# Block-2 key, value and gate-column weights loaded into another buffer than the weight ring

## The chip, the cores and the metric

The kernel runs on one core of a Trainium2 chip. The metric is the device time of one execution in microseconds (us). Weights are read from the chip's memory in single precision; nothing is resident between executions.

## What is computed

Two transformer-like blocks, one after the other, on 256 latent tokens of width 1024 (the first block also carries 256 context tokens). The change lies in the second block, which has two layers, each with weights of its own. Cut to what matters:

```
h = rms_norm_2(x, norm_mix[l]) * (1.0 + sc1) + sh1
proj = h @ w_in[l]                       # 1024 x 7440
dn_qkv, dn_z, dn_a, dn_b, sw_q, sw_k, sw_v, gate_a, gate_b = _split_columns(proj, IN_SIZES)
dn_qkv = silu(causal_dwconv(dn_qkv, dn_conv[l]))      # 3072 columns
g, beta = gates from dn_a, dn_b                       # 8 + 8 columns
o_dn = gated_delta_rule_chunked(dq, dk, dv, g, beta)
sq, sk = partial_rope(rms_norm_2(sw_q ...)), partial_rope(rms_norm_2(sw_k ...))
y_b = swa_sink_attention(sq, sk, sv, swa_sinks[l]) @ w_swa_out[l]    # sw_k, sw_v: 128 + 128 columns
merged = sigmoid(gate_a) * y_a + sigmoid(gate_b) * y_b
x = x + gt1 * (merged @ w_o[l])
x = x + gt2 * ((silu(up_act) * up_lin) @ w_down[l])
```

## The kernel before

The program of every engine is written out by hand, and engines meet only at semaphores. A planner (`make_plan`) walks the stages once and numbers two things: the *jobs* (one PSUM bank filled by TensorE and emptied by ScalarE or VectorE) and the *tiles* of the weight ring.

**The ring.** `ring` has two slots (`RING = 2`) of 2 MB each. A weight tile of a `weights` stage takes a whole slot, whatever its width; a weight tile of the feed-forward part takes half a slot. SyncE (SP) issues all weight loads in program order (`load`, L608 to L619). Before each load it waits until the tile that last filled the slot was used: for whole tiles, until the jobs of that tile are complete (`acc_full`). So the tile after next can be loaded only when the present one is finished. TensorE waits in `weights` (L708) until its slot has landed.

**The order in the second block.** Each layer begins with `norm`, and then, in this order: two query tiles of 512 columns (`swa_q`), the key tile of 128 columns (`swa_k`), the value tile of 128 columns (`swa_v`), six tiles of 512 columns for the delta rule (`dn_in`), and one tile of 16 columns (`dn_ab`). Queries, keys, values and the 16 columns go through `by_token` (TensorE line L763); the six tiles go through `by_feature` (L775), four blocks of 256 tokens each per tile, and VectorE convolves each block as it comes (L2710 to L2714). After that come the transposes (L1324), the attention with `dn_z` products filled in between (L789), and the rest of the layer. The layer ends with the feed-forward part (`seven_products`, TensorE line L724), which makes sums of the weights on VectorE (L2453 to L2456) and reads 22 up pairs and then 12 down chunks from half slots.

**Around the feed-forward part on SP.** After the loads of the 22 up pairs (`up_pairs`) SP issues eleven small loads of per-layer vectors (`layer_rows`) and then the down chunks (`down_chunks`), each of which waits for a half slot. For the first block's second feed-forward part these are the vectors of layer 0, for layer 0's they are those of layer 1.

**The slab buffer.** `mod_w`, 128 partitions of 2 x 2048 numbers, takes the slabs of the modulation matrices (SP line L598) while the first block runs; VectorE multiplies them (L2106) and counts them in `mod_used`. The last of the 88 slabs loaded there is used in the first block, before its second feed-forward part. Nothing in the second block touches `mod_w`.

Of the kernel before, what the change touches and what calls it, by code (L numbers as in the profile page):

```python
# [14 lines left out]
P = 128  # L15
D = 1024
KD = D // P
# [229 lines left out]
def make_plan():  # L247
    a = Plan()
    a.slab_tiles("modA", 2)
    a.free_jobs("xT", KD)  # L250
    a.slab_tiles("modA2", 2)
    a.free_jobs("norm0", 1)

    def tiles(where, stages, engine="A"):
        job = 0
        for name, jobs in stages:
            a.start(name)
            for n in jobs:
                for left in range(n, 0, -1):
                    a.add(name, engine[(n - left) % len(engine)])  # L260
                    if left == 1:
                        a.tile_used()
                    job += 1

    tiles("even", (("even_q", [4]), ("even_k", [4]), ("even_v", [4]), ("even_bi", [4]), ("even_bg", [4])))
    a.free_jobs("even_qkT", 2 * NT)
    a.use_banks(0, 1)
    for slot in range(SLOTS):
        for h, t in heads_at(slot):
            if t == 15:  # L270
                a.free_jobs(f"hg_o{h}", 1)
        for j, k in fill_at(slot):
            if (j, k) == (0, 0):
                a.start(f"head{slot // PER_ROUND}")
            if k == 0:
                a.add(f"head{slot // PER_ROUND}", "A")
            if (j, k) == (2, KD - 1):
                a.tile_used()
        if slot == CAT_SLOT:
            a.free_jobs("att_catT", KD // 2)  # L280
            a.start("even_out_a")
        if PART_SLOT <= slot < PART_SLOT + KD:
            a.add("even_out_a", "V")
            if slot == PART_SLOT + KD - 1:
                a.tile_used()
    a.use_banks(2, 3, 0, 1)
    a.free_jobs("hg_catT", KD // 2)
    a.weights("even_out", [KD], "V")
    first = a.tile["even_q"]
    a.slab_tile = [first + 2 * (3 * i // 2 // 4) for i in range(MOD_EARLY)] + [first + 2 * ((13 + i // 2) // 4) for i in range(KD)]  # L290
    a.free_jobs("norm1", 1)
    a.sevens("ffn0", "down0")
    a.slab_tile += [a.tile["ffn0"] + q - 1 for q in range(KF) for _ in range(up_slabs(q))]
    a.slab_tile += [a.tile["down0"] + n for n in range(4 * len(CHUNKS)) for _ in range(DOWN_SLABS[n])]
    a.free_jobs("norm2", 1)
    tiles("odd", (("ret_q", [4, 4]), ("ret_k", [4, 4]), ("ret_v", [4] * 4), ("ret_g", [2] * 4)))
    a.slab_tile += [a.tile["ret_q"] + n for n in (2, 2, 2, 2, 4, 4, 4, 4, 4, 6, 6, 6, 6, 6, 6, 8, 8, 8, 10, 10, 10, 12, 12, 12,
                                                  14, 14, 14, 16)]
    a.free_jobs("ret_oT", KD)
    a.pairs("ret_out", 1)  # L300
    a.free_jobs("norm3", 1)
    a.sevens("ffn1", "down1")
    assert len(a.slab_tile) == KD * (len(MOD_GROUPS) - 1)

    for l in range(2):
        a.free_jobs(f"norm@{l}", 1)
        a.weights(f"swa_q@{l}", [2, 2])
        a.weights(f"swa_k@{l}", [2])
        a.weights(f"swa_v@{l}", [2])
        a.weights(f"dn_in@{l}", [4] * 6, "V")  # L310
        a.weights(f"dn_ab@{l}", [2])
        a.free_jobs(f"swa_qkT@{l}", 6)
        a.weights(f"dn_z@{l}", [2, 2])
        a.free_jobs(f"swa_oT@{l}", KD)
        a.weights(f"swa_out@{l}", [2, 2])
        a.weights(f"gate_b@{l}", [2, 2])
        a.weights(f"gate_a@{l}", [2, 2])
        a.free_jobs(f"dn_oT@{l}", KD)
        a.weights(f"dn_out@{l}", [2, 2], "V")
        a.free_jobs(f"mergeT@{l}", KD)  # L320
        a.weights(f"w_o@{l}", [4, 4], "V")
        a.free_jobs(f"norm_ffn@{l}", 1)
        a.sevens(f"up@{l}", f"down@{l}")
    return a
# [39 lines left out]
def first_then_second_block(nc, a, out):  # L364
    pl = make_plan()
    DEPTH2 = a["w_in_2"].shape[0]

    with ExitStack() as ctx:
# [122 lines left out]
        def half_tile(n, k):  # L491

            return ring[:, n // 2 % RING, 2048 * (n % 2):2048 * (n % 2) + 256 * k].rearrange(
                "p (k e n) -> p k e n", e=2, n=256)

        rv, rg, rk, rq = view(0, 4, 2048), view(8192, 2, 2048), view(12288, 8, 512), view(16384, 8, 256)
        r_t = view(18432, 2, 2, 256)
        r_P, r_D, r_junk = view(19456, 2, 4, 256), view(21504, 2, 4, 256), gate[:, 0, 0:512]
# [30 lines left out]
        w_in = [sem(f"weights{s}_in") for s in range(RING)]  # L529
        h_in = [sem(f"half_weights{s}_in") for s in range(2 * RING)]  # L530
        w_part = sem("weights_partly_used")
        st_ws, st_ts = sem("st_weight_sums"), sem("st_input_sums")
        st_p1, st_p6, st_p7, st_p2, st_x, st_z = (sem(f"st_{n}") for n in (
            "product1", "product6", "product7", "product2", "x_full", "z_full"))
# [44 lines left out]
        def _(sp):  # L579
# [83 lines left out]
            for c in range(12):  # L663
                load(wcols(a["odd_w_in"][0], 512 * c, 512 * c + 512))
            down(a["odd_w_out"][0], (16,))
            up_pairs(a["ffn_w_in"][1])
            layer_rows(0)
            down_chunks(a["ffn_w_out"][1])
            for l in range(DEPTH2):
                w = a["w_in_2"][l]  # L670
                for lo, n in ((4112, 512), (4624, 512), (5136, 128), (5264, 128), (0, 512), (512, 512), (1024, 512),
                              (1536, 512), (2048, 512), (2560, 512), (4096, 16), (3072, 512), (3584, 512)):
                    load(wcols(w, lo, lo + n))
                for h in range(2):
                    load(wcols(a["w_swa_out_2"][l], 512 * h, 512 * h + 512))
                for lo in (6416, 6928, 5392, 5904):
                    load(wcols(w, lo, lo + 512))
                for name in ("w_dn_out_2", "w_o_2"):
                    for h in range(2):
                        load(wcols(a[name][l], 512 * h, 512 * h + 512))  # L680
                up_pairs(a["w_up_2"][l])
                if l + 1 < DEPTH2:
                    layer_rows(l + 1)
                down_chunks(a["w_down_2"][l])
            assert tile.n == pl.tiles and slab.n == len(pl.slab_tile)

# [8 lines left out]
        def _(pe):  # L695
# [57 lines left out]
                    if k == KD - 1:  # L753
                        fresh[0] = None

            def by_token(tiles, width, src=hT, where=None):

                w = weights(width)
                for i in tiles:
                    b = bank()  # L760
                    for k in range(KD):
                        first_use(k)
                        ins = nc.tensor.matmul(b[:, 0:width], src[:, k, P * i:P * (i + 1)], w[:, k, :],  # L763
                                               start=k == 0, stop=k == KD - 1)
                    ins.then_inc(acc_full, 1)
                    mod_after(where)
# [538 lines left out]
            for l in range(DEPTH2):  # L1305
# [2 lines left out]
                norm(4 + 2 * l, 256, "norm")  # L1308
                for _ in range(2):
                    by_token(LAT, 512)  # L1310
                for _ in range(2):
                    by_token(LAT, P)
                for _ in range(6):
                    by_feature(4, 256, 512)
                by_token(LAT, 16)

                stage("swa_qkT")
                for i in range(2):
# [1540 lines left out]
```

## Time and profile before

| what | value |
|---|---|
| median of 3 executions | 2884.79 us (2884.76, 2884.79, 2913.66) |
| profiled execution | 2885.55 us, of which the span is 2883.4 us |
| mean granted TensorE clock in the profiled execution | 0.969 of full speed |
| TensorE busy | 2720.8 us, 94% of the span |
| VectorE busy | 1542.3 us, 53% |
| ScalarE busy | 669.5 us, 23% |
| moved from the chip's memory | 383.96 MB, 134 GB/s over the span |

The span is the time from the first to the last recorded event of one profiled execution. All other times are read in it as us from its start. A busy TensorE isn't TensorE at its peak: in some stretches the clock granted to it is half of the full one, and then the same work keeps it busy for twice as long.

### The profile page before, as it was taken

What the parts mean: (1) busy time and instruction counts of PE and PEld (TensorE: products, weight loads), DVE (VectorE), ACT (ScalarE), POOL (GpSimd) and SP (SyncE); (2) the same over time, 40 slices, a digit from 0 to 9 for tenths busy, and PEclk for the clock granted to TensorE, in tenths of its full rate; (3) what the DMA queues carried; (4) which work ended last, traced back from release to release, by engine and by line L of the source; (5) the groups of instructions that cost most, each with busy time, mean ns of one, the idle gap of its engine ahead of it and who ended that gap; (6) DMA issues with size and microseconds to landing.
All of it is one profiled execution on the core that took longest, in us unless ns stands there. A gap on an engine that the chain in (4) does not pass through costs nothing.

```text
span 2883.4 us, 36232 instructions
## 1 busy us (share of the span) xinstructions
PE 2720.8 (94%) x14426; PEld 2050.3 (71%) x14426; DVE 1542.3 (53%) x3100; ACT 669.5 (23%) x1727; POOL 0.2 (0%) x4
## 2 busy tenths in 40 slices
PE   6899988999999999899999999989998999998999
PEld 2445555888887444589977756668996864775999
DVE  4856555755775521136745554425773654443775
ACT  3134322111102100212111351222311144222330
POOL 0000000000000000000000000000000000000000
PEclk9998889999999999999999999999999999999999
DMA  7530012555475844145634221124553322113554
GB/s 291 200 94 23 34 55 88 175 161 171 174 282 199 304 165 163 59 130 164 181 131 151 97 88 59 59 88 130 164 182 127 134 88 88 59 59 101 154 168 134
DMA packets 336164, 387.36 MB, mean 134 GB/s; under 512 B 10988, under 2 KB 265084, under 8 KB 323452
## 3 DMA queue, kind: packets, MB, share of 16 engines
q1 hardware_dynamic: 333260, 378.15, 39.9%
q10 hardware_dynamic: 2736, 6.89, 0.7%
q8 instruction: 115, 1.88, 0.3%
q14 instruction: 53, 0.43, 0.0%
HBM read 383.96 MB, written 1.05 MB: 134 GB/s over the span
## 4 chain that ended last, share of the span: by engine, by line
PE 86%; DVE 6%; DMA 3%; ACT 3%; issue 2%; ACTq 0%; SPq 0%; DVEq 0%
PE acc L724 24%; PE acc L763 12%; PE acc L775 11%; PE mx L724 10%; PE acc L789 8%; PE acc L1031 2%; PE acc L1016 2%; PE acc L805 2%; PE mx L1409 1%; PE mx L1398 1%; PE mx L1407 1%; DVE arena L2106 1%; PE mx L889 1%; PE mx L1291 1%; PE acc L821 1%
## 5 line engine op out<-in xcount | busy, mean ns | idle before, releaser
L763 PE MATMUL acc<-ring,hT 128*128 128x512 f32 (+2 forms) x1152 | 407.6, 515 | 19.3 <-DMA ring<-in_even_w_in 9.5
L763 PEld LDWEIGHTS acc<-ring,hT 128*128 128x128 f32 x1152 | 197.9, 194 | 226.2 <-issue 207.6
L724 PE MATMUL acc<-arena 128*128 128x128 f32 (+1 forms) x2056 | 322.6, 299 | 2.1 <-ACT gate L1817 0.8
L775 PE MATMUL acc<-hT,ring 128*128 128x256 f32 (+1 forms) x1280 | 311.5, 407 | 12.8 <-DMA ring<-in_w_in 8.1
L775 PEld LDWEIGHTS acc<-hT,ring 128*128 128x128 f32 x1280 | 246.9, 193 | 76.5 <-issue 33.8
L724 PEld LDWEIGHTS acc<-arena 128*128 128x128 f32 x2056 | 282.8, 192 | 16.1 <-ACT gate L1817 1.4
L2106 DVE SCALAR_TENSOR_TENSOR arena<-mod_w,vcols,arena 128x2048 f32<-128x2048 f32 x98 | 228.4, 2348 | 110.4 <-DMA mod_w<-in_w_ada 100.9
L789 PE MATMUL acc<-ring,hT 128*128 128x512 f32 x512 | 258.0, 625 | 1.1 <-ACT hT L1496 1.1
L724 PE MATMUL acc<-hT,ring 128*128 128x128 f32 (+1 forms) x1208 | 194.9, 311 | 12.1 <-ACT hT L1586 12.0
L2453 DVE TENSOR_TENSOR arena<-ring 128x512 f32<-128x512 f32 (+1 forms) x136 | 91.6, 674 | 192.6 <-PE acc L724 184.7
L724 PEld LDWEIGHTS acc<-hT,ring 128*128 128x128 f32 x1208 | 171.6, 197 | 26.5 <-issue 11.8
L724 PE MATMUL acc<-arena,ring 128*128 128x128 f32 (+1 forms) x1160 | 182.4, 300 | 1.9 <-DVE x L2594 1.9
L724 PEld LDWEIGHTS acc<-arena,ring 128*128 128x128 f32 x1160 | 159.7, 192 | 10.4 <-DVE x L2594 2.7
L1496 ACT ACTIVATE arena<-acc 128x512 f32<-128x512 f32 (+2 forms) x136 | 69.8, 527 | 414.2 <-PE acc L763 293.4
L789 PEld LDWEIGHTS acc<-ring,hT 128*128 128x128 f32 x512 | 91.4, 196 | 89.7 <-issue 84.4
L724 PE MATMUL mx<-hT,ring 128*128 128x128 f32 (+1 forms) x928 | 151.0, 307 | 0.0
L724 PE MATMUL mx<-arena,ring 128*128 128x128 f32 (+1 forms) x928 | 148.5, 302 | 0.0
L724 PEld LDWEIGHTS mx<-hT,ring 128*128 128x128 f32 x928 | 132.5, 196 | 6.5
L724 PEld LDWEIGHTS mx<-arena,ring 128*128 128x128 f32 x928 | 128.7, 191 | 9.0 <-issue 3.4
L724 PE MATMUL acc<-hT,arena 128*128 128x128 f32 (+1 forms) x760 | 124.7, 307 | 0.0
L724 PEld LDWEIGHTS acc<-hT,arena 128*128 128x128 f32 x760 | 108.3, 191 | 6.0
L1031 PE MATMUL acc<-hT,ring 128*128 128x512 f32 x192 | 99.7, 659 | 0.0
(355 smaller groups left out, 3441.0 us busy)
## 6 DMA issues: line engine op xcount, KB each, us to landing
ring<-in_w_in SPq DMA_DIRECT2D x28, 2048.0 KB
mod_w<-in_w_ada SPq DMA_DIRECT2D x48, 1024.0 KB, 5.9
ring<-in_ffn_w_in SPq DMA_DIRECT2D x88, 512.0 KB
ring<-in_w_up SPq DMA_DIRECT2D x88, 512.0 KB
mod_w<-in_mod_w SPq DMA_DIRECT2D x40, 1024.0 KB, 5.0
ring<-in_odd_w_in SPq DMA_DIRECT2D x12, 2048.0 KB
ring<-in_ffn_w_out SPq DMA_DIRECT2D x16, 1024.0 KB
ring<-in_w_down SPq DMA_DIRECT2D x16, 1024.0 KB
```

The source lines that it names most:

```text
L724: ins = nc.tensor.matmul(out, w[:, k, :], h[:, k, :], start=start and k == 0, stop=stop and k == n - 1, skip_group_check=more)
L763: ins = nc.tensor.matmul(b[:, 0:width], src[:, k, P * i:P * (i + 1)], w[:, k, :], start=k == 0, stop=k == KD - 1)
L775: ins = nc.tensor.matmul(b[:, 0:hi - lo], w[:, k, P * f:P * (f + 1)], hT[:, k, lo:hi], start=k == 0, stop=k == KD - 1)
L789: ins = nc.tensor.matmul(filling.b, src[:, k, P * i:P * (i + 1)], filling.w[:, k, :], start=k == 0, stop=k == KD - 1)
L805: ins = nc.tensor.matmul(b[:, 0:width], w[:, k, P * f:P * (f + 1)], src[:, at + k, :], start=at + k == 0, stop=at + k == sum(groups) - 1)
L821: ins = nc.tensor.transpose(b[:, at:at + P], src[:, i, P * (k + q):P * (k + q + 1)], ident)
L889: nc.tensor.matmul(mx[:, u % 2, 0:P * blocks], q, k, start=True, stop=True).then_inc(att_s, 1)
L1016: ins = nc.tensor.matmul(b, w[:, k, P * f:P * (f + 1)], hT[:, first + k, :], start=k == 0, stop=k == 3)
L1031: ins = nc.tensor.matmul(hb, hw[:, kk, P * j:P * (j + 1)], hT[:, kk, :], start=kk == 0, stop=kk == KD - 1)
L1496: ins = nc.scalar.activation(dst, src, func, **kw)
L2106: ins = V.scalar_tensor_tensor(acc_, mod_w[:, i % 2, :], vcols[:, at:at + 1], acc_, ALU.mult, ALU.add)
L2453: V.tensor_tensor(s3, a11, a10, ALU.subtract)
```

## The change

The key and value columns of one layer, which are neighbours in `w_in`, are loaded by one transfer of 128 x 8 x 256 numbers (1 MB) into the first half of `mod_w`, and the 16 gate columns by one of 128 x 8 x 16 numbers (64 KB) into its second half. Both are issued by SP at the previous feed-forward part, between its up pairs and its down chunks: for layer 0 ahead of the small vectors, for layer 1 behind them. TensorE waits for a semaphore of their own (`small_in`) once a layer, ahead of the key product. The three ring tiles of each layer are gone; the jobs, the products and the order of TensorE's work stay.

```diff
@@ make_plan
-        a.weights(f"swa_k@{l}", [2])
-        a.weights(f"swa_v@{l}", [2])
+        a.free_jobs(f"swa_k@{l}", 2)
+        a.free_jobs(f"swa_v@{l}", 2)
         a.weights(f"dn_in@{l}", [4] * 6, "V")
-        a.weights(f"dn_ab@{l}", [2])
+        a.free_jobs(f"dn_ab@{l}", 2)
@@ views
+        kv_w = mod_w[:, 0, :].rearrange("p (k n) -> p k n", k=KD)
+        ab_w = mod_w[:, 1, 0:P].rearrange("p (k n) -> p k n", k=KD)
@@ SP
+            def small_weights(l):
+                if l:
+                    sp.wait_ge(acc_full, pl.own[f"dn_ab@{l - 1}"][-1] + 1)
+                else:
+                    sp.wait_ge(mod_used, KD * (len(MOD_GROUPS) - 1))
+                sp.dma_start(kv_w, wcols(a["w_in_2"][l], 5136, 5392)).then_inc(small_in, 16)
+                sp.dma_start(ab_w, wcols(a["w_in_2"][l], 4096, 4112)).then_inc(small_in, 16)
             up_pairs(a["ffn_w_in"][1])
+            small_weights(0)
             layer_rows(0)
             down_chunks(a["ffn_w_out"][1])
...
-                for lo, n in ((4112, 512), (4624, 512), (5136, 128), (5264, 128), (0, 512), (512, 512), (1024, 512),
-                              (1536, 512), (2048, 512), (2560, 512), (4096, 16), (3072, 512), (3584, 512)):
+                for lo, n in ((4112, 512), (4624, 512), (0, 512), (512, 512), (1024, 512),
+                              (1536, 512), (2048, 512), (2560, 512), (3072, 512), (3584, 512)):
                     load(wcols(w, lo, lo + n))
...
                 if l + 1 < DEPTH2:
                     layer_rows(l + 1)
+                    small_weights(l + 1)
@@ TensorE
-                for _ in range(2):
-                    by_token(LAT, P)
+                pe.wait_ge(small_in, 32 * l + 32)
+                for v in range(2):
+                    by_token(LAT, P, w=kv_w[:, :, P * v:P * (v + 1)])
                 for _ in range(6):
                     by_feature(4, 256, 512)
-                by_token(LAT, 16)
+                by_token(LAT, 16, w=ab_w)
```

SP's queue at layer 0, from the last load of a query tile on (`in_w_in_2` is the matrix `w_in` of the second block; 128x8x512 is a 2 MB tile, 128x8x128 the key or value tile, 128x8x16 the gate columns). Before:

```order
L616 DMA ring<-in_w_in_2 128x8x512 [waits st_down_product,weights_partly_used]
L616 DMA ring<-in_w_in_2 128x8x128 [waits acc_full] x2
L616 DMA ring<-in_w_in_2 128x8x512 [waits acc_full] x6
L616 DMA ring<-in_w_in_2 128x8x16 [waits acc_full]
L616 DMA ring<-in_w_in_2 128x8x512 [waits acc_full] x2
L616 DMA ring<-in_w_swa_out_2 128x8x512 [waits acc_full] x2
```

And after the change:

```order
L619 DMA ring<-in_w_in_2 128x8x512 [waits st_down_product,weights_partly_used]
L619 DMA ring<-in_w_in_2 128x8x512 [waits acc_full] x8
L619 DMA ring<-in_w_swa_out_2 128x8x512 [waits acc_full] x2
```

The first `dn_in` tile now stands directly behind the second query tile, so that it waits for the jobs of the first query tile and no longer for those of the key tile.

SP's queue in the first block's second feed-forward part, at the end of the up pairs (`in_ffn_w_in`) and the start of the down chunks (`in_ffn_w_out`), after the change:

```order
L619 DMA ring<-in_ffn_w_in 128x8x128
L674 DMA mod_w<-in_w_in_2 128x8x256 [waits mod_slabs_used]
L675 DMA mod_w<-in_w_in_2 128x8x16
L657 DMA prow<-in_dn_conv_2 96x128
...
L661 DMA brow<-in_dn_norm_2 128x128
L619 DMA ring<-in_ffn_w_out 128x8x256 [waits st_z_full] x2
```

The two rows with `mod_w` are new; before, the row with `prow` followed the up pair directly.

## Rows read from the trace of the kernel before

**Rows 1.** The page: its span, TensorE's busy time, the chain by engine.

```profile
span 2883.4 us, 36232 instructions
PE 2720.8 (94%) x14426; PEld 2050.3 (71%) x14426; DVE 1542.3 (53%) x3100; ACT 669.5 (23%) x1727; POOL 0.2 (0%) x4
PE 86%; DVE 6%; DMA 3%; ACT 3%; issue 2%; ACTq 0%; SPq 0%; DVEq 0%
```

**Rows 2.** Waits of TensorE from 1495 us on: total us, times, longest us.

```profile
PE mx L1367 <- DVE arena L2767: 10.3, 2, 5.1
...
PE acc L775 <- DMA ring<-in_w_in: 8.1, 2, 4.4
...
PE acc L763 <- DMA ring<-in_w_in: 0.9, 2, 0.4
```

**Rows 3.** Timeline of TensorE, start of layer 0: start, us, what, [idle before <-releaser].

```profile
1495.04 33.99 PE L763 MATMUL acc<-ring,hT 128*128 128x512 f32 x96 [2.16 <-ACT hT L1586]
1529.45 3.84 PE L763 MATMUL acc<-ring,hT 128*128 128x128 f32 x32 [0.41 <-DMA ring<-in_w_in]
1536.98 84.83 PE L775 MATMUL acc<-hT,ring 128*128 128x256 f32 x384 [3.69 <-DMA ring<-in_w_in]
1621.65 3.64 PE L763 MATMUL acc<-ring,hT 128*128 128x16 f32 x32
```

**Rows 4.** Timeline of TensorE, start of layer 1.

```profile
2225.49 3.84 PE L763 MATMUL acc<-ring,hT 128*128 128x128 f32 x32 [0.45 <-DMA ring<-in_w_in]
2233.75 84.83 PE L775 MATMUL acc<-hT,ring 128*128 128x256 f32 x384 [4.42 <-DMA ring<-in_w_in]
```

**Rows 5.** Timeline of SP at layer 0, issues without their waits.

```profile
1511.81 0.39 SPq L616 DMA_DIRECT2D ring<-in_w_in  x1
...
1525.54 3.96 SPq L616 DMA_DIRECT2D ring<-in_w_in  x2
```

**Rows 6.** Windows around the two waits: stretch, us, busy by engine, PEclk, DMA share, GB/s.

```profile
1533.30:1537.00 3.70, 0.02 (x1) 0.02 (x1) 0.00 (x0) 3.40 (x5) 0.00 (x0) 1.00 1.06 392
1537.00:1540.00 3.00, 3.00 (x10) 2.45 (x11) 0.00 (x0) 0.00 (x0) 0.00 (x0) 0.68 1.05 390
1540.00:1543.00 3.00, 3.00 (x12) 2.55 (x11) 0.54 (x2) 0.00 (x0) 0.00 (x0) 0.75 0.53 194
...
2233.80:2236.80 3.00, 3.00 (x9) 2.42 (x10) 0.00 (x0) 0.00 (x0) 0.00 (x0) 0.60 1.04 388
2236.80:2239.80 3.00, 3.00 (x13) 2.59 (x12) 0.57 (x2) 0.00 (x0) 0.00 (x0) 0.83 0.29 104
```

**Rows 7.** Windows: a 2 MB tile, the gate columns, first down chunks with the pause ahead.

```profile
1595.20:1601.40 6.20, 6.20 (x31) 5.45 (x30) 3.18 (x8) 0.83 (x2) 0.00 (x0) 1.00 0.96 338
1609.00:1610.00 1.00, 1.00 (x7) 0.87 (x6) 0.93 (x3) 0.00 (x0) 0.00 (x0) 1.00 0.70 66
1405.80:1408.50 2.70, 2.70 (x27) 2.70 (x26) 1.46 (x6) 0.55 (x2) 0.00 (x0) 1.00 0.13 29
1408.50:1413.00 4.50, 4.50 (x42) 4.50 (x42) 3.62 (x6) 0.86 (x4) 0.00 (x0) 1.00 0.73 245
2103.70:2107.70 4.00, 4.00 (x38) 4.00 (x37) 3.17 (x8) 1.44 (x4) 0.00 (x0) 1.00 0.77 261
```

**Rows 8.** Timeline of VectorE: convolution of the first two dn_in blocks, layer 0.

```profile
1542.43 0.48 DVE L2710 TENSOR_SCALAR arena<-acc,pcols 128x256 f32<-128x256 f32 x1 [9.24 <-PE acc L775]
...
1545.88 0.48 DVE L2710 TENSOR_SCALAR arena<-acc,pcols 128x256 f32<-128x256 f32 x1 [1.42 <-PE acc L775]
```

**Rows 9.** Timeline of VectorE: first use of the first down chunk, both feed-forward parts.

```profile
1415.85 0.68 DVE L2453 TENSOR_TENSOR arena<-ring 128x512 f32<-128x512 f32 x1
...
2112.16 0.68 DVE L2453 TENSOR_TENSOR arena<-ring 128x512 f32<-128x512 f32 x1
```

**Rows 10.** Timeline of TensorE: its first product with the first down chunk.

```profile
1418.94 1.06 PE L724 MATMUL mx<-arena,ring 128*128 128x128 f32 x8
```

**Rows 11.** Windows of one place in layer 0 and its counterpart in layer 1.

```profile
1730.00:1742.00 12.00, 9.65 (x20) 4.86 (x20) 3.12 (x14) 1.55 (x7) 0.00 (x0) 0.72 0.01 1
2427.00:2439.00 12.00, 9.65 (x27) 4.58 (x27) 3.90 (x16) 2.14 (x8) 0.00 (x0) 1.00 0.04 3
```

More of the change, by code:

```diff
@@ L531, in first_then_second_block @@
         w_part = sem("weights_partly_used")
+        small_in = sem("small_weights_in")
         st_ws, st_ts = sem("st_weight_sums"), sem("st_input_sums")
@@ L754, in first_use, with by_token @@
                         fresh[0] = None
-            def by_token(tiles, width, src=hT, where=None):
-                w = weights(width)
+            def by_token(tiles, width, src=hT, where=None, w=None):
+                w = weights(width) if w is None else w
                 for i in tiles:
```

## The prediction

> **What bounds the kernel now.** I read the page first. TensorE is busy for 94% of the span and carries 86% of the chain that ended last [rows 1]. So time comes back only where TensorE stands idle or runs at a low clock, and the next view is the list of what it waited for. In the second block, the waits for weights in the ring are 8.1 us ahead of L775, in two pieces, and 0.9 us ahead of L763, in two pieces [rows 2]. The larger entry ahead of them, 10.3 us, is a wait for VectorE in the delta rule; the change doesn't touch it.
>
> Then the timeline says where the pieces are. In layer 0 the query products start at 1495.04. The key product follows them without a pause. The value product, at 1529.45, had to wait 0.41 us for its tile. It ends at 1533.29, and then TensorE stands for 3.69 us until the first `dn_in` tile has landed at 1536.98 [rows 3]. Layer 1 shows the same, with 0.45 and 4.42 us [rows 4]. The product of the 16 gate columns, at 1621.65, had no wait at all [rows 3].
>
> SP's queue says why. At 1511.81, when the first query tile is used up, it issues the key tile. At 1525.54, when the second is used up, it issues the value tile, and the next issue in that row ends at 1525.54 + 3.96 = 1529.50 [rows 5]: this is the first `dn_in` tile, which had to wait until the key jobs were complete. From 1529.5 to 1536.98 are 7.5 us for 2 MB, and the transfer engines run at their full share meanwhile (1.06 at 392 GB/s) [rows 6]. Nothing is slow there. The load starts too late, because a 0.5 MB tile held a 2 MB slot.
>
> **Part 1: the three tiles leave the ring.** The first `dn_in` tile now waits for the first query tile, so it is issued at 1511.8. A 2 MB tile takes 6.2 us of transfer [rows 7]; with the 7.5 us from issue to landing seen above it is there at 1519.3. It is needed when the value product ends, at 1533.3 less 0.4. That leaves some 13 us. The second tile is issued when the second query tile is used up, at 1525.5, and lands at 1533.0, while its turn comes 13.8 us after the first tile's start (four blocks of 3.45 us: VectorE gets the first at 1542.43 and the second at 1545.88 [rows 8]). So it has some 13 us too. From there on each tile has 13.8 us for a load of 7.5. The waits of 3.69 and 0.41 us go whole, and nothing in the ring is late next.
>
> **Part 2: the clock behind the wait.** TensorE's granted clock is 1.00 during the wait of 3.7 us, and then 0.68 and 0.75 in the two stretches of 3 us behind it: part of the time it ran at the lower level (1.2 of 2.4 GHz). What this lost is 3 x 0.32 + 3 x 0.25 = 1.71 us. In layer 1 it is 3 x 0.40 + 3 x 0.17 = 1.71 us [rows 6]. With the wait gone TensorE is busy without a pause from 1495.04 on, and I take it that the clock stays up. VectorE's start fits this: the first block took 1542.43 - 1536.98 = 5.45 us against 3.45 for the next [rows 8], of which the 1.71 is the greater part.
>
> **Part 3: who else must keep up.** VectorE waited 9.24 us ahead of the first block and 1.42 us ahead of the second [rows 8]. It needs 2.0 us of each 3.45, so it follows an earlier TensorE. Every later wait in the layer is one of an engine for another's work that itself begins earlier. They move with TensorE and don't grow. The gate columns cost nothing before and cost nothing after.
>
> **Part 4: the added loads.** In both feed-forward parts SP issues two more transfers, at some 0.39 us each as in [rows 5], 0.8 us in all, and the transfer engines move 1.06 MB more. The nearest row for the 1 MB is the first down chunk, of the same shape and size: at 245 GB/s over 4.5 us (3.3 us of full share) [rows 7]. The gate columns took 0.7 of 1 us at 66 GB/s [rows 7]. Together this is 4.0 us of transfer per layer, queued ahead of the first down chunk, whose issue moves by 0.8 us as well. That chunk landed by 1413.0 and VectorE first read it at 1415.85 [rows 7, 9]; in layer 0's part it landed by 2107.7 and was read at 2112.16 [rows 7, 9]. So it has 2.9 and 4.5 us to spare before anyone starts later. In the first case the transfer engines were nearly idle for 2.7 us before the chunk (share 0.13 [rows 7]), and this absorbs most of the 4.0 us; in both, TensorE's own first use is 3.1 us behind VectorE's (1418.94 [rows 10]). The lower bound of the cost is therefore nothing, and the upper is the whole of what exceeds the spare time with no gap absorbed: 4.8 - 2.9 = 1.9 us once and 0.3 us once, 2.2 us in all. I take nothing, since VectorE's lead over TensorE stands behind the first margin. The new waits on SP (the slabs used, the gate jobs of layer 0 complete) were met long before; nothing is queued behind them that would feel it. TensorE's new wait for `small_in` comes some 120 us after the issue.
>
> On the DMA order, the Trainium skill (DMA: Bandwidth & Descriptors, Queues, rings and completion order) says that each DMA engine takes the descriptors of one ring in their order. By that rule the down chunk must indeed stand behind the whole 1.06 MB, which is how the bound above is drawn; by a rule without order it would be less.
>
> **The sum.** Layer 0: 0.41 + 3.69 + 1.71 = 5.81 us. Layer 1: 0.45 + 4.42 + 1.71 = 6.58 us. Together 12.4 us. The profiled execution took 2885.55 us, 0.8 us above the median of 2884.79. Against its own time the changed kernel would take 2873.2; I give the forecast against the median: 2884.8 - 12.4 = 2872.4 us.
>
> **Rivals.**
> *The clock falls elsewhere.* The loss at low clock is not tied to the program alone. At one place in layer 0 (1730 to 1742) the mean clock is 0.72, at its counterpart in layer 1 (2427 to 2439) it is 1.00, with the same 9.65 us of busy time in the same 12 us [rows 11]. That is 12 x 0.28 = 3.4 us in one and none in the other. If all that follows begins 5 to 12 us earlier, such places can change sides. About ten pauses follow; with one or two changed by 3.4 us or by half of it, the forecast moves by up to 5 us to either side: 2867 to 2878. That all of them go one way and eat half of the gain or more (2878 to 2882), or add as much (2863 to 2867), is possible too. For it speaks the pair of rows; against it, that flips should cancel. The Trainium skill (TensorE: Matmul & The Clock Gate, The HAM clock gate) says that the check of activity runs freely and isn't reset by the kernel; by that rule a shift alone re-deals these losses, and the trace agrees, as far as one pair of places can show.
>
> *The wait moves.* If the first `dn_in` tile were no longer late but something behind it were, for instance VectorE, which also norms and rotates the queries between the blocks, part of the 8.1 us would return. Half of it back gives 2884.8 - 6 = 2879. Against it speaks that TensorE has no wait of size between 1536.98 and 1621.65 (84.83 us in one piece [rows 3]).
>
> *Slower.* The early loads could hold up the down chunks. The point from which this decides: to end above the old time the two chunks must together cost TensorE more than 12.4 us, so each must land some 6 us beyond its spare time, that is 9 to 11 us later than now, for 4.8 us of added queue. It needs transfers of 1 KB pieces and 64 byte pieces at a third to a half of the speed in [rows 7]. Then 2885 to 2890.
>
> *The change doesn't do what it says.* The first `dn_in` tile would have to wait for something other than the first query tile's jobs. The order of SP's queue excludes it as far as I see. Then 2884.8.
>
> **How the numbers follow.** Forecast with its clock spread, 2867 to 2878: 0.74. The clock takes or adds more, 2863 to 2867 or 2878 to 2882: 0.16. The wait moves, 2878 to 2883: 0.05. Slower: 0.03. No effect: 0.02. A range of 2866 to 2879 holds about eight in ten: the first case, the near edges of the second, and the upper bound of 2.2 us for the added loads. One per cent is 28.8 us, and within about that a measurement of this kernel can't tell a change from none. Only faster by 28.8 or slower by as much would be told apart; the sum of all waits for ring tiles here is 9 us. So: faster 0.01, same 0.97, slower 0.02.
>
> **What the changed kernel's profile would show.** Right: no DMA wait ahead of L775's and L763's counterparts in the second block; the `dn_in` products start within 0.1 us of the value product's end, at 1532.9 and near 2223; the clock is 1.00 there; VectorE gets the first block some 3.6 us after its products start, and not 5.45. The first down chunk lands 1 to 4 us later relative to the up pairs, and no engine waits for it. Wrong: a DMA entry ahead of L2453's or L724's counterparts near 1416 or 2112; a clock below 1.00 in the first `dn_in` tile though there was no pause; or the later stages losing what was won. What would upset the figure itself is mostly the clock.

## The result and the profile after

| | kernel before | changed kernel |
|---|---|---|
| executions | 17 | 17 |
| median | 2884.79 us (2876.93 to 2913.66) | 2874.6 us (2859.93 to 2882.72) |
| profiled execution | 2885.55 us, mean clock 0.969 | 2874.6 us, mean clock 0.967 |

The ratio of the changed kernel to the one before is 0.9931, 95% interval [0.9905, 0.9958]: 19.9 us less (12.1 to 27.4), a time of 2864.9 on the old median. The medians differ by 10.2 us. So the sign and the order of size are as forecast (12.4 us), and the forecast ratio, 0.9957, lies just inside the interval; but by the ratio the time is 1.1 us below the forecast's range. The means differ by 14.0 us (a ratio of 0.9952). So three ways of comparing give 10, 14 and 20 us. Between the first two stand three long executions of the kernel before (2905.74 to 2913.66); the ratio on record lies beyond both, and how it weighs the executions isn't on record.

The page of the changed kernel, its span and the chain by engine, beside [rows 1]:

```profile
span 2872.5 us, 36220 instructions
PE 2720.3 (95%) x14426; PEld 2051.1 (71%) x14426; DVE 1543.2 (54%) x3100; ACT 670.2 (23%) x1727; POOL 0.2 (0%) x4
PE 85%; DVE 6%; DMA 3%; ACT 3%; issue 2%; SPq 0%; ACTq 0%; DVEq 0%
```

TensorE is as long busy as before, to 0.5 us. The timeline of TensorE at the start of layer 0 and of layer 1 (start, us, what, idle before it), beside [rows 3, 4]. L776 is the old L763, and L788 the old L775:

```profile
1496.06 29.61 PE L776 MATMUL acc<-ring,hT 128*128 128x512 f32 x64 [2.17 <-ACT hT L1600]
1525.50 7.31 PE L776 MATMUL acc<-mod_w,hT 128*128 128x128 f32 x64
1532.65 83.05 PE L788 MATMUL acc<-hT,ring 128*128 128x256 f32 x384
1615.53 3.64 PE L776 MATMUL acc<-mod_w,hT 128*128 128x16 f32 x32
...
2214.54 7.31 PE L776 MATMUL acc<-mod_w,hT 128*128 128x128 f32 x64
2221.69 83.05 PE L788 MATMUL acc<-hT,ring 128*128 128x256 f32 x384
```

No row has an idle time before it except the first. The four waits for the ring, 9.0 us in [rows 2], are gone, and no DMA stands any longer among what TensorE waited for in the second block. The `dn_in` products take 83.05 us in place of 84.83: the 1.8 us of low clock behind each wait is gone too. The windows of that place have the full clock, beside [rows 6]:

```profile
1532.00:1535.00 3.00, 3.00 (x19) 2.74 (x18) 1.36 (x2) 2.09 (x4) 0.00 (x0) 1.00 0.19 68
1535.00:1538.00 3.00, 3.00 (x15) 2.64 (x15) 1.59 (x4) 1.31 (x2) 0.00 (x0) 1.00 0.00 0
```

Two things are new. The first is in the feed-forward part of the first block. SP's timeline there, after the change:

```profile
1399.31 1.02 SPq L619 DMA_DIRECT2D ring<-in_ffn_w_in  x2
1400.37 1.12 SPq L674 DMA_DIRECT2D mod_w<-in_w_in  x1
1401.53 1.77 SPq L675 DMA_DIRECT2D mod_w<-in_w_in  x1
1403.34 2.21 SPq L657 DMA_DIRECT2D prow<-in_dn_conv  x1
...
1409.80 2.42 SPq L619 DMA_DIRECT2D ring<-in_ffn_w_out  x2
```

The same stretch of the kernel before has the up pair and then the small vectors at once, and the down chunk (`in_ffn_w_out`) was issued at 1405.79:

```profile
1399.48 1.02 SPq L616 DMA_DIRECT2D ring<-in_ffn_w_in  x2
1400.54 1.01 SPq L654 DMA_DIRECT2D prow<-in_dn_conv  x1
1401.59 0.32 SPq L654 DMA_DIRECT2D prow<-in_norm_mix  x1
```

The two new issues took 1.12 and 1.77 us, not 0.39, and the one behind them 2.21 in place of 1.01. The down chunk was issued 4.0 us later. In layer 0's part it is otherwise. There the small vectors stand ahead, the transfer engines are nearly idle (shares of 0.17 and 0.05 from 2093 to 2095), and the same two issues are short (SP's timeline after the change):

```profile
2093.94 0.43 SPq L674 DMA_DIRECT2D mod_w<-in_w_in  x1
2094.41 0.58 SPq L675 DMA_DIRECT2D mod_w<-in_w_in  x1
```

From the issue of the last up pair to that of the first down chunk it is 7.3 us there (2087.72 to 2095.04), and 6.4 before (2095.17 to 2101.57): 0.9 us more. VectorE and TensorE felt the added loads in both parts (timelines of the changed kernel; L2467 is the old L2453 of [rows 9], L737 the old L724):

```profile
1418.36 0.69 DVE L2467 TENSOR_TENSOR arena<-ring 128x512 f32<-128x512 f32 x1 [2.60 <-DMA ring<-in_ffn_w_out]
...
2106.67 0.69 DVE L2467 TENSOR_TENSOR arena<-ring 128x512 f32<-128x512 f32 x1 [1.87 <-DMA ring<-in_w_down]
...
1422.19 1.16 PE L737 MATMUL acc<-arena,ring 128*128 128x128 f32 x8 [0.58 <-DVE arena L2516]
...
2111.12 1.16 PE L737 MATMUL acc<-arena,ring 128*128 128x128 f32 x8 [1.10 <-DVE arena L2516]
```

So 1.7 us of the 9.0 are given back.

The second is the clock. Taken over windows of 1 us, busy time times (1 - granted clock) sums to 78.9 us in the profile before and to 78.8 us after. In this pair, the 3.4 us that went behind the two waits came back elsewhere: one place in layer 1 that had 3.4 us has 6.5 now. This window of the changed kernel shows it, with 0.54 over 15 us:

```profile
2308.00:2323.00 15.00, 14.30 (x38) 7.30 (x39) 3.40 (x14) 6.81 (x21) 0.00 (x0) 0.54 0.25 96
```

The same place in the kernel before, 18 us later in its span, has 0.77:

```profile
2326.00:2341.00 15.00, 14.95 (x43) 7.36 (x43) 7.34 (x33) 5.38 (x25) 0.00 (x0) 0.77 0.36 131
```

Followed through the two profiles: the changed kernel is 1.0 us behind when the queries of layer 0 start (1496.06 against 1495.04), 4.3 ahead at the `dn_in` products of layer 0 and 12.1 ahead at those of layer 1 (2221.69 against 2233.75). With the 1.8 us that these products are shorter it is 13.8 ahead, and at the end of the span 10.9. The rest of layer 1 gave 2.9 us back; by the windows it has 13.0 us of low clock in place of 8.2. The terms of the pair, 9.0 us of waits gone, 1.7 given back and 0.1 of clock, make 7.2 of the 10.95 us; the other 3.7 I can't put down to single rows.

### The profile page after: what moved, and what is told of

Same layout as the page of the kernel before. It is cut to its first block, busy times and chain, and to the rows that moved or that the text cites. A ratio compares the mean times of both kernels' runs of the same rounds, so it can differ in the third digit from the quotient of the medians.

```text
span 2872.5 us, 36220 instructions
## 1 busy us (share of the span) xinstructions
PE 2720.3 (95%) x14426; PEld 2051.1 (71%) x14426; DVE 1543.2 (54%) x3100; ACT 670.2 (23%) x1727; POOL 0.2 (0%) x4
## 4 chain that ended last, share of the span: by engine, by line
PE 85%; DVE 6%; DMA 3%; ACT 3%; issue 2%; SPq 0%; ACTq 0%; DVEq 0%
PE acc L737 23%; PE acc L776 13%; PE acc L788 11%; PE mx L737 10%; PE acc L802 8%; PE acc L1044 2%; PE acc L1029 2%; PE acc L818 2%; PE mx L1423 2%; PE mx L1412 1%; PE mx L1421 1%; DVE arena L2120 1%; PE mx L902 1%; PE mx L1304 1%; PE acc L834 1%
## 5 line engine op out<-in xcount | busy, mean ns | idle before, releaser
L776 PE MATMUL acc<-ring,hT 128*128 128x512 f32 (+1 forms) x960 | 384.1, 562 | 17.7 <-DMA ring<-in_even_w_in 8.7
L776 PEld LDWEIGHTS acc<-ring,hT 128*128 128x128 f32 x960 | 175.2, 194 | 222.4 <-issue 202.7
L737 PE MATMUL acc<-arena 128*128 128x128 f32 (+1 forms) x2056 | 322.6, 299 | 2.1 <-ACT gate L1831 0.8
L788 PE MATMUL acc<-hT,ring 128*128 128x256 f32 (+1 forms) x1280 | 307.8, 403 | 4.7 <-ACT hT L1600 3.4
L737 PEld LDWEIGHTS acc<-arena 128*128 128x128 f32 x2056 | 282.8, 192 | 16.0 <-ACT gate L1831 1.4
L788 PEld LDWEIGHTS acc<-hT,ring 128*128 128x128 f32 x1280 | 244.5, 191 | 67.0 <-issue 33.9
L737 PE MATMUL acc<-hT,ring 128*128 128x128 f32 (+1 forms) x1208 | 194.5, 311 | 12.1 <-ACT hT L1600 12.1
L2467 DVE TENSOR_TENSOR arena<-ring 128x512 f32<-128x512 f32 (+1 forms) x136 | 91.7, 675 | 196.4 <-PE acc L737 183.9
L737 PEld LDWEIGHTS acc<-hT,ring 128*128 128x128 f32 x1208 | 171.2, 197 | 26.5 <-issue 11.8
L737 PE MATMUL acc<-arena,ring 128*128 128x128 f32 (+1 forms) x1160 | 182.9, 300 | 3.8 <-DVE x L2608 2.1
L737 PEld LDWEIGHTS acc<-arena,ring 128*128 128x128 f32 x1160 | 159.8, 192 | 12.6 <-DVE x L2608 2.9
L802 PEld LDWEIGHTS acc<-ring,hT 128*128 128x128 f32 x512 | 91.4, 196 | 89.7 <-issue 84.7
L737 PE MATMUL mx<-hT,ring 128*128 128x128 f32 (+1 forms) x928 | 151.0, 307 | 0.0
L737 PE MATMUL mx<-arena,ring 128*128 128x128 f32 (+1 forms) x928 | 148.5, 302 | 0.0
L737 PEld LDWEIGHTS mx<-hT,ring 128*128 128x128 f32 x928 | 132.5, 196 | 6.5
L737 PEld LDWEIGHTS mx<-arena,ring 128*128 128x128 f32 x928 | 128.7, 191 | 9.0 <-issue 3.4
L737 PE MATMUL acc<-hT,arena 128*128 128x128 f32 (+1 forms) x760 | 124.7, 307 | 0.0
L737 PEld LDWEIGHTS acc<-hT,arena 128*128 128x128 f32 x760 | 108.3, 191 | 6.0
```

The costliest lines, as they stand in the source:

```text
L737: ins = nc.tensor.matmul(out, w[:, k, :], h[:, k, :], start=start and k == 0, stop=stop and k == n - 1, skip_group_check=more)
L788: ins = nc.tensor.matmul(b[:, 0:hi - lo], w[:, k, P * f:P * (f + 1)], hT[:, k, lo:hi], start=k == 0, stop=k == KD - 1)
L802: ins = nc.tensor.matmul(filling.b, src[:, k, P * i:P * (i + 1)], filling.w[:, k, :], start=k == 0, stop=k == KD - 1)
L2467: V.tensor_tensor(s3, a11, a10, ALU.subtract)
```

## The experiments

The theory: the gain is the four waits for ring tiles, because a narrow tile holds a whole slot; each with low clock behind it. The rivals: the clock decides the size; the early loads cost something or nothing; something else in the ring's order gives the gain.

Every execution comes with its mean granted clock. So a second figure is given beside the ratio: the time multiplied by the mean clock, as if the whole had run at full clock. The clock is known to 0.001, that is to 1.4 us for one execution. The mean of such products with its 95% interval is called *the time at full clock*. It shows what a change does apart from the clock, and so it can't show whether a change also gains by the clock; for that the clocks themselves have to be compared. It also counts low clock while TensorE stands idle, which costs nothing. Executions at a clock under 0.962 are left out of it (16 of the kernel before in the third series, 3 of gate columns only, and 1 of the longer wait at 0.961; see the upper group, below). A kernel is compared with the one before of its own series: the second series ran on one chip, the third on another, and for the kernel before in the first series no clocks are on record. The changed kernel itself isn't in the third series. The second series goes down to the ring tile of 256, the third from there on.

| run | executions | median us | ratio [95%] | clock | time at full clock |
|---|---|---|---|---|---|
| changed kernel, first series | 17 | 2874.6 | 0.9931 [0.9905, 0.9958] | 0.968 | 2781.3 +- 1.8 |
| before, second series | 17 | 2885.4 | | 0.967 | 2790.5 +- 1.2 |
| changed kernel again | 6 | 2871.4 | 0.9954 [0.9942, 0.9967] | 0.9685 | 2782.8 +- 4.9 |
| keys and values only | 5 | 2864.2 | 0.9932 [0.9919, 0.9945] | 0.971 | 2782.7 +- 2.5 |
| wait put back | 11 | 2888.0 | 1.0005 [0.9995, 1.0014] | 0.967 | 2791.7 +- 2.3 |
| one ring tile of 256 | 5 | 2869.0 | 0.9946 [0.9935, 0.9958] | 0.969 | 2781.4 +- 2.0 |
| before, third series | 35 | 2887.0 | | 0.969 (19 of 35) | 2789.9 +- 1.0 |
| loads later | 12 | 2863.5 | 0.9909 [0.9868, 0.9950] | 0.970 | 2781.3 +- 2.1 |
| gate columns only | 12 | 2883.7 | 0.9994 [0.9944, 1.0043] | 0.968 | 2789.7 +- 1.9 |
| longer wait | 12 | 2886.6 | 0.9977 [0.9938, 1.0016] | 0.968 | 2796.3 +- 1.3 |
| double load | 12 | 2875.8 | 0.9945 [0.9905, 0.9984] | 0.969 | 2786.2 +- 1.8 |

**The changed kernel again.** No edit.

> The changed kernel once more, beside its variants. First theory (the late first dn_in tile): 9.0 us of waits gone, some 0.6 to 1 us given back in front of the down chunks, and the low clock behind the two waits (1.7 us each) gone at its place; 10 to 14 us below the kernel before, and the two waits missing in the profile. Rival (the clock decides the size): the loss at low clock summed over the profile stays what it was before, 78 us, since it only moves to other pauses; then 8 to 9 us in the mean, and single executions 10 us apart because their clocks differ.

Measured: 13.3 us less (9.5 to 16.7), in a series in which all 17 executions of the kernel before lay within 2879 and 2890. At full clock it is 7.7 us below before, and the first series' figure lies 9.2 below the same one, which is of another series: 9.0 less 1.7 is 7.3. Its profile has 74.9 us of low clock, 3.9 less than the first. The first theory's range holds. That part of the gain which exceeds the waits is the clock's, but it is a gain: the means differ by 12.0 us, and the rival's 8 to 9 aren't met.

**Keys and values only.** The gate columns keep a ring tile.

```diff
-        a.free_jobs(f"dn_ab@{l}", 2)
+        a.weights(f"dn_ab@{l}", [2])
-                      (1536, 512), (2048, 512), (2560, 512), (3072, 512), (3584, 512)):
+                      (1536, 512), (2048, 512), (2560, 512), (4096, 16), (3072, 512), (3584, 512)):
-                by_token(LAT, 16, w=ab_w)
+                by_token(LAT, 16)
```

> Only the key and value columns leave the ring; the 16 gate columns keep their ring tile in both layers. First theory: the gate columns' tile never made anyone wait, so the time is that of the changed kernel within 1 us and no wait comes back. Rival (the gate columns' slot matters, since it delays the first dn_z tile by one tile): a wait for weights appears where the attention begins and 1 us or more of the gain is missing.

Measured: 19.4 us below before in the mean, and 7.4 below the changed kernel, which neither expected. At full clock it is the same as the changed kernel (2782.7 against 2782.8). The difference is its clock: 0.971 in the mean, and 65.2 us of low clock in its profile. One wait for a ring tile has appeared where the attention begins, of 0.9 us, as the rival said, and VectorE's waits for the down chunks are shorter, 0.3 and 1.3 us in place of 2.3 and 1.7. The two about cancel.

**The wait put back.** SP holds the first `dn_in` tiles as long as the ring did before.

```diff
+                    if lo in (0, 512):
+                        sp.wait_ge(acc_full, pl.own[f"swa_{'v' if lo else 'k'}@{l}"][-1] + 1)
                     load(wcols(w, lo, lo + n))
```

> The changed kernel, but SP holds the first dn_in tile until the key jobs are complete and the second until the value jobs are, as the ring did before; the early loads stay. First theory: the waits of 3.7 and 4.4 us are back in front of the first dn_in products with 1.7 us of low clock behind each, and the time is that of the kernel before, up to 1 us above it less the 0.9 us of the two value waits. Rival (the gain comes from something else in the change, such as fewer or larger transfers): it keeps a good part of the gain, 5 us or more.

Measured: the whole gain is gone, ratio 1.0005. Timeline of TensorE at both layers (L790 is the old L775):

```profile
1535.23 84.83 PE L790 MATMUL acc<-hT,ring 128*128 128x256 f32 x384 [4.28 <-DMA ring<-in_w_in]
...
2235.10 84.83 PE L790 MATMUL acc<-hT,ring 128*128 128x256 f32 x384 [4.73 <-DMA ring<-in_w_in]
```

9.0 us of waits, and the products take 84.83 us again, to the hundredth. At full clock it is 1.2 us above before, which fits the 1.7 us of the early loads, though the interval of 2.3 is wider. The rival, that something else in the change gives the gain, falls.

**A longer wait.** Both tiles held until the value jobs are complete.

```diff
-                        sp.wait_ge(acc_full, pl.own[f"swa_{'v' if lo else 'k'}@{l}"][-1] + 1)
+                        sp.wait_ge(acc_full, pl.own[f"swa_v@{l}"][-1] + 1)
```

> A double dose of the wait: the changed kernel, with both the first and the second dn_in tile held until the value jobs are complete. That is 3.7 us later than in the run with the old waits put back, so waits of some 7.5 us per layer in place of 4.5. First theory: 7 to 8 us above that run (2888.0), 2895 to 2897, plus up to 2 us where the clock falls for longer. Rival (these waits are only a part of why the kernel is slower, the rest is a fixed cost of the ring's order): less than 5 us above it.

Measured: waits of 7.6 and 7.8 us in front of the same products, 6.4 more than with the wait put back, and 5.2 us more at full clock, each against the kernel before of its own series (6.4 and 1.2 us above). In plain times, without the execution at 2897.7, it is 8.3 us above the mean of before's lower group, and the other was 1.7 above: 6.6 us more. A microsecond of this wait costs about a microsecond. The first theory's 7 to 8 was slightly high. The rival's figure, less than 5, was just passed, by less than the intervals. The expected 2895 to 2897 weren't reached: the median is 2886.6, below that of the run with the wait put back, because before's lower group lies lower in this series too (2879.3 in the mean against 2885.3).

```profile
1535.84 85.18 PE L790 MATMUL acc<-hT,ring 128*128 128x256 f32 x384 [7.59 <-DMA ring<-in_w_in]
...
2238.64 85.36 PE L790 MATMUL acc<-hT,ring 128*128 128x256 f32 x384 [7.77 <-DMA ring<-in_w_in]
```

Here the products take 85.2 and 85.4 us, so the low clock behind a wait nearly twice as long costs only 0.4 to 0.5 us more.

**Gate columns only.** Keys and values stay in their two tiles.

```diff
-        a.free_jobs(f"swa_k@{l}", 2)
-        a.free_jobs(f"swa_v@{l}", 2)
+        a.weights(f"swa_k@{l}", [2])
+        a.weights(f"swa_v@{l}", [2])
-                sp.dma_start(kv_w, wcols(a["w_in_2"][l], 5136, 5392)).then_inc(small_in, 16)
```

> Only the 16 gate columns leave the ring; keys and values keep their two tiles. First theory: no gain, the waits ahead of the value product (0.4 us) and of the first dn_in tile (3.7 and 4.4 us) stay as before; within 1 us of the kernel before. Rival (freeing the ring helps wherever it is freed): 1 us or more below it.

Measured: ratio 0.9994, at full clock 0.2 us below before, and the waits ahead of `dn_in` are there (8.0 us). This part of the change gives nothing that shows: the ratio alone leaves some 14 us to either side, the time at full clock about 2.

**One ring tile of 256 columns.** The kernel before, with keys and values in one tile, nothing early and `mod_w` unused.

```diff
-        a.weights(f"swa_k@{l}", [2])
+        a.free_jobs(f"swa_k@{l}", 2)
         a.weights(f"swa_v@{l}", [2])
-                for lo, n in ((4112, 512), (4624, 512), (5136, 128), (5264, 128), (0, 512), ...
+                for lo, n in ((4112, 512), (4624, 512), (5136, 256), (0, 512), ...
-                for _ in range(2):
-                    by_token(LAT, P)
+                kv_w = weights(256)
+                for v in range(2):
+                    by_token(LAT, P, w=kv_w[:, :, P * v:P * (v + 1)])
```

> The kernel before, but keys and values are one ring tile of 256 columns in place of two of 128; the slab buffer isn't used and nothing is loaded early. The first dn_in tile is then issued when the second query tile is used up, at 1525.5, and needs 7.5 us, so it lands at 1533.0, when the value product ends. First theory: waits of 0 to 1 us are left and the low clock behind them is mostly gone, so 10 to 13 us below the kernel before, without the wait of VectorE in front of the down chunks. Rival (taking the tiles out of the ring altogether matters): at least 4 us above the changed kernel.

Measured: 15.6 us less (12.1 to 18.8), at full clock 9.1 below before, as good as the changed kernel. Its timeline:

```profile
1531.85 83.15 PE L775 MATMUL acc<-hT,ring 128*128 128x256 f32 x384 [0.77 <-DMA ring<-in_w_in]
...
2220.81 83.15 PE L775 MATMUL acc<-hT,ring 128*128 128x256 f32 x384 [0.74 <-DMA ring<-in_w_in]
```

Two waits of 0.75 us are left, without low clock behind them, and there is no wait in front of the down chunks. The rival falls: it isn't needed to leave the ring, only not to give 128 columns a slot of their own.

**Loads later.** The new transfers stand ahead of the third of the four groups of down chunks.

```diff
             def down_chunks(w, small=None):
                 for p in range(4):
                     at = 0
+                    if p == 2 and small is not None:
+                        small_weights(small)
```

> The changed kernel, but SP issues the key, value and gate-column transfers in the middle of the down chunks (ahead of the third of their four groups) in place of ahead of the first. In the changed kernel's profile VectorE waits 2.6 us for the first down chunk and TensorE 0.6 and 1.1 us behind it. First theory: these waits go and no other comes, so 1 to 2 us below the changed kernel at equal clock. Rival (the early load costs nothing, and those pauses are the clock's or chance): the same time as the changed kernel, within 1 us.

Measured: no DMA is left in VectorE's or TensorE's list of waits behind 1300 us, so the 1.7 us are gone in the profile. The times don't resolve it: 2781.3 at full clock, the changed kernel 2781.3 and 2782.8. Its ratio is the best of all, 0.9909 [0.9868, 0.9950], with a clock of 0.970; I don't call it faster than its neighbours. It does beat the kernel before, by any figure.

**Double load.** A third transfer of 0.94 MB behind the other two; nobody reads it.

```diff
+                sp.dma_start(spare_w, wcols(a["w_in_2"][l], 5392, 5632)).then_inc(small_in, 16)
-                pe.wait_ge(small_in, 32 * l + 32)
+                pe.wait_ge(small_in, 48 * l + 48)
```

> The changed kernel with a third transfer of 0.94 MB into the spare part of the slab buffer behind the other two, in both feed-forward parts; nobody reads it. This doubles the load ahead of the first down chunk, some 2.8 us more of transfer. First theory: VectorE's wait for the first down chunk grows by 2.5 to 4 us in both places and TensorE stands 2 to 4 us longer in each, 4 to 8 us above the changed kernel. Rival (the early load is covered): within 1 us of it.

Measured: 4.2 us above the average of the changed kernel's two figures at full clock, which are of the other series; against the kernel before it gains 3.7 us, where the changed kernel gained 7.7. The waits of VectorE for the first down chunk are 6.4 and 4.2 us, and TensorE now waits for the chunk itself (rows from the lists of waits; total, times, longest):

```profile
PE mx L739 <- DMA ring<-in_ffn_w_out: 3.2, 1, 3.2
...
PE mx L739 <- DMA ring<-in_w_down: 1.6, 1, 1.6
PE acc L739 <- DVE arena L2518: 1.6, 1, 1.6
DVE arena L2469 <- DMA ring<-in_ffn_w_out: 6.4, 1, 6.4
DVE arena L2469 <- DMA ring<-in_w_down: 4.2, 1, 4.2
```

That is 6.4 us of TensorE's, 4.7 more than in the changed kernel. The cover in front of the down chunks is used up by the change; the prediction's "slower" rival is a real mechanism, at some 2.4 us per added 0.94 MB and layer.

**Four more profiles of the kernel before.** No edit. (What the first expectation calls the second series is the third of the table.)

> The kernel before, unchanged, for one more profile. Of 35 of its executions in the second series 16 took 2908 to 2914 us at a mean clock of 0.955 to 0.959 and 19 took 2873 to 2888 at 0.966 to 0.971; none of 64 executions of kernels that have the key and value columns out of their two ring tiles was in the upper group. If this profile is of the upper group, it shows where some 30 us of low clock lie. First theory (the clock is re-dealt at pauses, place by place): many pauses of the second block with 3.4 us of low clock where the lower group has 1.7 or none. Rival (one long stretch): the clock stays at the lower level in one stretch of 30 to 60 us. Since the first block is the same in all kernels, both expect the difference behind 1400 us.

> The same once more, with the same expectation; two profiles of the lower group would show how far the places with low clock differ between executions of one kernel: by the first theory the total stays within 76 to 82 us and the places of the first block agree better than those of the second.

> The kernel before once more, for a profile of its upper group (2908 to 2914 us, mean clock 0.955 to 0.959), which the two last profiles were not. The same expectation: many pauses with more low clock behind 1400 us by the first theory, one long stretch at the lower level by the rival.

> A fourth profile of the kernel before, again for its upper group; the expectation is that of the run ahead of it: many pauses with more low clock, or one long stretch.

Measured: 2878.4, 2875.5, 2891.3 and 2887.1 us, with 72.1, 71.7, 82.2 and 82.2 us of low clock; the first profile had 2885.6 and 78.9. The time less the low clock is 2803.8 to 2809.1 in all five, so of 15.8 us between the fastest and the slowest 10.5 are low clock. The changed kernel's two profiles, read so, have 2795.8 and 2795.3, some 10.6 us less than the mean of the five; the longer wait has 2813.2 and the double load 2802.1. The wait put back has 2803.6, at the lower edge of the five. The expectation of 76 to 82 us was too narrow. The places change too. This is the window of layer 1's place of [rows 11] in the third of the four:

```profile
2427.00:2439.00 12.00, 9.64 (x20) 4.78 (x20) 3.26 (x14) 1.55 (x8) 0.00 (x0) 0.72 0.00 0
```

It has 0.72 where [rows 11] have 1.00, at the same work in the same microseconds. Of the differences a part lies ahead of 1400 us, where all kernels do the same: the fourteen profiles have 39.4 to 47.3 us of low clock there. None of the four was of the upper group, so what that group is stays open.

## Why the prediction was right, and where it failed

**What bounds it, and part 1.** Right. The four waits of 9.0 us went whole, nothing in the ring was late next, and putting the waits for the two tiles back puts the whole time back (1.0005).

**Part 2, the clock behind the wait.** Right at the place (83.05 us for 84.83), and of the wrong size for the whole. The profiled pair shows no gain at all, 78.9 before and 78.8 after. Over many executions there is one: in the second series the three kernels without the wait (one of them with 0.75 us of it left) have a mean clock of 0.9694 in 16 executions, and the two with it (before, and the wait put back) 0.9671 in 28. The difference of 0.0023 (0.001 to 0.0035) is some 6.5 us, between 3 and 10, by an estimate that counts the idle stretches too, where 3.4 had been put into the sum. In the third series it is 0.9695 in 24 executions against 0.9689 in before's lower group, 1.7 us and not clear of the scatter. The profiles fit a gain of this size but are few: 73.5 us of low clock on average in the six without the wait, 78.9 in the eight with it.

**Part 3.** Right; no other wait of the second block grew.

**Part 4, the added loads.** The cost was taken as nothing, with a bound of 2.2 us; TensorE lost 0.58 and 1.10 us. So the bound held, but the sign named for being wrong came true: VectorE waited for the first down chunk in both parts. Two sizes failed. In the first block's part it was SP's issue time, taken from a row at an idle queue (0.39 us); with an up pair in transfer the two issues took 1.12 and 1.77 us and held up the next, 4.0 us in all in place of 0.8. In layer 0's part the issues held the chunk up by only 0.9 us, but it was there 6.4 us later behind the last up pair (18.95 us in place of 12.53), so that some 5.5 us went to the transfers ahead of it, for which 4.0 had been taken. The margin of 2.9 us went mostly by the issues, that of 4.5 mostly by the transfers. That the loss stayed small is as argued: VectorE's lead stood behind the margin.

**The sum and the range.** 12.4 us was forecast, the ratio says 19.9 (12.1 to 27.4) and the repetition 13.3 (9.5 to 16.7); the forecast is inside both. The range missed the first by 1.1 us. That the repetition comes so near is in part luck: 1.7 us were lost that stood at nothing, and the clock gave some 4 us in place of its 3.4.

The step that failed is the size of the clock's term: 3.4 us in the sum, with 5 us to either side for the first rival, *the clock falls elsewhere*, on the likeliest course and 10 at the most. The waits were right (9.0 us, less 1.7 given back), so whatever goes beyond 7.3 us has to be sought elsewhere, and as far as the runs show it, it is the clock. They showed this in place of 3.4 us:

- Kernels without the wait have more clock in the mean, by some 6.5 us in the second series and 1.7 in the third, as above.
- Executions of one kernel differ by 10 us in low clock (71.7 to 82.2 in five profiles). Kernels that do the same work differ in their mean clock: 0.971 for keys and values only, 0.9685 for the changed kernel, which is 7 us, with five and six executions.
- The kernel before has an upper group of executions, 2908 to 2914 us at a clock of 0.955 to 0.959: 3 of 17 in the first series by their times (2905.7 to 2913.7), 16 of 35 in the third, none in the second. The 16 are 32.7 us over the lower group's mean; times their clock they come to 2787.0 us, so that the excess is low clock. The prediction has no such group. Gate columns only had 3 of 12 there. In the third series the three kernels with the key and value columns out of their two tiles had none in 36 (the nearest was 2897.7 us at 0.961, with the longer wait). So the waits alone don't make the group. Their other 44 executions, none of them there either, say less: the kernel before had few or none in those series.

Without the three upper executions of the first series the means are 9.3 us apart, and with them 14.0, so the group is worth 4.7 us there. The remaining 5.9 us up to the ratio's 19.9 stay open, as its weighing isn't on record; and what the group is stays open too.

## What to carry to other kernels

In a ring whose slots are released one by one, as this one's are, a tile that is used up quickly costs the load of the next large one; look for the wait one tile behind the narrow one, and first try to merge narrow tiles, which gave the same here without another buffer. A load "hidden" in an earlier stage must be priced by the queue it enters: the same two issues took 1.12 and 1.77 us with an up pair in transfer, and 0.43 and 0.58 without. And where a kernel's time has a spread from the granted clock, count the waits as the sure part of a gain and give the clock a range of its own. Times multiplied by their clock show the first part; the second shows only in the clocks of many executions.

## What was unexpected of the hardware

- The mean granted clock, known per execution, explains most of the spread between executions of one program: 0.957 at 2912 us against 0.969 at 2879 us in one series of the kernel before. The times multiplied by the clock are 2787.0 and 2789.9.
- Low clock comes mostly in pieces that cost about 1.7 or 3.4 us, behind a pause of TensorE, and the same pause at the same microsecond has it in one execution and not in another (0.72 against 1.00 over 12 us). The Trainium skill (TensorE: Matmul & The Clock Gate, The HAM clock gate) says that the activity check runs freely and isn't reset by the kernel; these rows agree.
- In total it was 65.2 to 89.0 us of some 2870 in the fourteen profiles of this study, 2.3 to 3.1%.
- How long the same DMA issues kept SP differed with what was in transfer: with an up pair ahead the new 1 MB and 64 KB loads took 1.12 and 1.77 us and the next small one 2.21; with the transfer engines at shares of 0.17 and 0.05 the first two took 0.43 and 0.58 us.
